# Squares added up on VectorE, norm statistics with tokens on partitions, modulation in pairs of blocks and partly inside the first FFN

## What is computed

```python
def rmsnorm(x, g):
    y = x * lax.rsqrt(jnp.mean(x * x, axis=-1, keepdims=True) + EPS)
    return y * g
def ada_mod(c, w, b, n):
    m = jax.nn.silu(c) @ w + b
    return m.reshape(c.shape[0], n, 1, D_MODEL)
# in every layer, m = ada_mod(...)
h = rmsnorm(x, g[0]) * (1.0 + m[:, 1]) + m[:, 0]
o = rglru_block(h, ...) or nsa_mix(h, ...)          # ends with a projection
x = x + m[:, 2] * rmsnorm(o, g[1])
h = rmsnorm(x, g[2]) * (1.0 + m[:, 4]) + m[:, 3]
o = conv_ffn(h, ...)                                # ends with a projection
x = x + m[:, 5] * rmsnorm(o, g[3])
```

## Time and profile before

| | us |
|---|---|
| median of three runs | 3645.05 (3637.66 to 3645.62) |
| the profiled execution | 3638.49 |
| its span | 3636.6 |
| PE, DVE, POOL, ACT busy | 3221.3, 1728.4, 1113.0, 968.8 |

### The profile page before, as it was taken

How to read it: one execution, slowest core, us unless ns; L and a number is a source line. 1 busy time by engine, 2 the same in 40 slices (tenths; PEclk the granted TensorE clock), 3 DMA queues, 4 the chain that set the end, 5 groups by cost and what they waited for, 6 DMA issues and landing times. The chain is left out here.

```text
span 3636.6 us, 58098 instructions
## 1 busy us (share of the span) xinstructions
PE 3221.3 (89%) x23056; PEld 2903.7 (80%) x23056; DVE 1728.4 (48%) x3136; ACT 968.8 (27%) x1534; POOL 1113.0 (31%) x799
## 2 busy tenths in 40 slices
PE   6886979999999988879767999889787999999986
PEld 5885959999999986879644666566677999999985
DVE  4666046454454445331278888700126454454454
ACT  4544033121121113112123777600123111111111
POOL 1232203333333331223012555400222333333330
PEclk9997989999999998999888999999899999999998
DMA  4213431111111124421242000066202111111112
GB/s 182 74 49 106 153 140 63 47 47 47 47 47 47 47 90 147 155 93 35 70 128 78 2 2 2 2 217 218 88 18 87 48 47 49 44 47 47 47 56 87
DMA packets 75786, 272.89 MB, mean 75 GB/s; under 512 B 9306, under 2 KB 19938, under 8 KB 73330
## 3 DMA queue, kind: packets, MB, share of 16 engines
q1 hardware_dynamic: 73810, 262.99, 20.9%
q10 hardware_dynamic: 1728, 6.34, 0.4%
HBM read 245.47 MB, written 33.10 MB: 77 GB/s over the span
## 5 line engine op out<-in xcount | busy, mean ns | idle before, releaser
L1424 POOL TENSOR_TENSOR w_hi<-w_raw,misc 128x1024 fp32r<-128x1024 f32 x197 | 381.8, 1938 | 2042.9 <-DMA w_raw<-in_w 780.3
L1426 POOL TENSOR_TENSOR w_lo<-w_raw,w_hi 128x1024 fp32r<-128x1024 f32 x197 | 496.6, 2521 | 28.4 <-issue 0.4
L1629 PE MATMUL PA<-hB_hi,w_hi 128*128 128x344 f32 x1512 | 327.5, 325 | 48.4 <-DVE hB_lo L613 23.2
L1629 PE MATMUL PB<-hB_hi,w_hi 128*128 128x344 f32 x1488 | 318.2, 322 | 20.6 <-DVE hB_lo L1813 18.0
L1629 PE MATMUL PB<-hB_lo,w_hi 128*128 128x344 f32 x1488 | 316.8, 321 | 18.0 <-POOL w_lo L1426 18.0
L1629 PE MATMUL PA<-hB_lo,w_hi 128*128 128x344 f32 x1512 | 324.2, 323 | 0.0
L1629 PE MATMUL PA<-hB_hi,w_lo 128*128 128x344 f32 x1416 | 301.5, 322 | 0.0
L1629 PEld LDWEIGHTS PA<-hB_hi,w_hi 128*128 128x128 f32 x1512 | 256.7, 190 | 54.7 <-issue 23.7
L385 DVE SCALAR_TENSOR_TENSOR zb<-ub,vec,zb 128x1024 f32<-128x1024 f32 x48 | 157.9, 3289 | 294.5 <-ACT zb L357 294.5
L1629 PE MATMUL PB<-hB_hi,w_lo 128*128 128x344 f32 x1392 | 294.3, 320 | 0.0
L1629 PEld LDWEIGHTS PB<-hB_hi,w_hi 128*128 128x128 f32 x1488 | 250.9, 189 | 24.1 <-issue 18.2
(11 more groups left out here) (439 smaller groups left out, 6368.7 us busy)
## 6 DMA issues: line engine op xcount, KB each, us to landing
w_raw<-in_w SPq DMA_DIRECT2D x197, 512.0 KB, 3.5
pages<-in_pages SPq DMA_DIRECT2D x64, 384.0 KB, 4.2
cosT<-in_mw SPq DMA_DIRECT2D x32, 512.0 KB, 3.5
sinT<-in_mw SPq DMA_DIRECT2D x32, 512.0 KB, 4.4
mt<-in_mw SPq DMA_DIRECT2D x32, 512.0 KB, 3.9
x_dram<-X SPq DMA_DIRECT2D x3, 4128.0 KB, 12.1
X<-x_dram SPq DMA_DIRECT2D x3, 4128.0 KB, 13.3
mw<-in_mw SPq DMA_DIRECT2D x4, 2048.0 KB, 22.6
```

Source lines behind the costliest of these rows:

```text
L1424: pool.tensor_tensor(w_hi[b], w_raw[b], zero.broadcast_to([P, 1024]), ALU.add)
L1426: pool.tensor_tensor(w_lo[b], w_raw[b], w_hi[b].bitcast(F32), ALU.subtract).then_inc(sem("w_split"), 1)
L1629: mm = pe.matmul(PS[ps][:, c, 0:CH], w[:, w0:w0 + P], x[:, k, c * CH:(c + 1) * CH], start=(k == 0 and n == 0), stop=(k == K - 1 and n == 2))
```

## The change

The odd norms are redone. ACT squares each output block as it comes (`square`, straight from PSUM in the two projections), DVE adds the squares to one accumulator (`acc_add`), and after the last block PE multiplies 9 chunks of 128 tokens of the accumulator with one column of ones (`stats`). The sums then stand with tokens on partitions, 128x9 elements; root and reciprocal are taken of these, and nine transposes of a broadcast column spread them over the partitions in PSUM, from where `residual` reads them. The even norms stay.

Modulation goes in pairs of blocks: one load of 1 MB, passes of 256 columns, one ACT copy, two folds. There is one load buffer and one row buffer. Pairs 0 to 7 run in the LRU loop, 8 to 11 after the first four tiles of the LRU's output projection, 12 to 31 in FFN 0 (one after each pair of up tiles, chunks 0 to 4), 32 to 47 in stage C. The window after the LRU loop and those around norms 1 to 4 go.

The weight loads of the LRU loop are issued a turn ahead. Stage C works only on the 8(i+1) blocks of 64 that query tile i can see, clears the rest of its buffers once, and takes the guard against an empty sum for i = 0 alone. The five copies are issued by ACT after stage C. `ident` is loaded at the start.

```diff
-    def rows_of(pe, e, landed, bank, cs=csil, tiles=mt):
-        pe.wait_ge(sem(f"mt_in{e}"), landed)
+    def rows_of(pe, landed, bank, cs=csil, tiles=mt):
+        pe.wait_ge(sem("mt_in"), landed)
         for k in range(KT):
             q = 32 * (k % 4)
-            mm = pe.matmul(bank[q:q + 32, 0:P], cs[:, NC * k:NC * k + 32], tiles[e][:, k * P:(k + 1) * P],
-                           start=(k < 4), stop=(k >= 4), skip_group_check=True)
+            mm = pe.matmul(bank[q:q + 32, 0:2 * P].rearrange("p (e n) -> p e n", n=P), cs[:, NC * k:NC * k + 32],
+                           tiles[:, :, k * P:(k + 1) * P], start=(k < 4), stop=(k >= 4), skip_group_check=True)
...
+    def ffn_mod(pe, c, p):
+        n = c * PAIRS + (p + 12)
+        pe.wait_ge(sem("md_ev"), n)
+        rows_of(pe, n * 16 + 16, PC)
...
+    def mod_load(sp, p, tiles=mt):
+        after(sp, sem("md_rows"), p)
...
+    def square(act, n, k, src):
+        if k >= 3:
+            act.wait_ge(sem("acc_added"), 7 * (n // 2) + k - 2)
+        out = sq_of(n, k)
+        act.activation(c3(out) if src.ndim == 3 else out, src, ACT.Square).then_inc(sem("nsq_ready"), 1)
+    def acc_add(dve, n, k):
+        dve.wait_ge(sem("nsq_ready"), 8 * (n // 2) + k + 1)
+        dve.drain()
+        acc = sq_of(n, 0)
+        dve.tensor_tensor(acc, acc, sq_of(n, k), ALU.add).then_inc(sem("acc_added"), 1)
+    def stats(pe, n, evicted):
+        pe.wait_ge(*evicted)
+        pe.wait_ge(sem("acc_added"), 7 * (n // 2) + 7)
+        for c in range(KT + 1):
+            t = min(c * P, TOK - P)
+            mm = pe.matmul(PA[:, 0, c:c + 1], acc[:, t:t + P], ones[:, 0:1], start=True, stop=True, skip_group_check=True)
+        mm.then_inc(sem("col_sums"), 1)
+        pe.wait_ge(sem("rst_ready"), n // 2 + 1)
+        for c in range(KT + 1):
+            mm = pe.transpose(PB[:, c // 4, c % 4 * P:(c % 4 + 1) * P], rst[:, c:c + 1].broadcast_to([P, P]), ident)
+        mm.then_inc(sem("rms_spread"), 1)
...
         def root(n):
-            act.wait_ge(sem("sq_used"), 8 * n + 8)
-            act.activation(c3(rms), PA[:, :, 0:CH], ACT.Sqrt, bias=deps).then_inc(sem("sqrt_done"), 1)
+            act.wait_ge(sem("col_sums"), n // 2 + 1)
+            act.activation(rst, PA[:, 0, 0:KT + 1], ACT.Sqrt, bias=deps).then_inc(sem("sqrt_done"), 1)
...
-                    dve.tensor_tensor(b[f"t{k % 2}_{NREG[n]}"][:, 0:NPR], src[:, k, 0:NPR], rms[:, 0:NPR], ALU.mult)
+                    dve.tensor_tensor(b[f"t{k % 2}_{NREG[n]}"][:, 0:NPR], src[:, k, 0:NPR], flat(PB[:, 0:2, :]), ALU.mult)
...
+                for p in range(1, PAIRS):
+                    stream(t0 + 2 * p, t0 + 2 * p + 2)
+                    mod_load(sp, 12 + p)
+                def chunk(c):
+                    for n in range(12):
+                        tile_load((c - 1) * 12 + (t0 + 8 + n), n % 2)
+                        if n in (1, 3, 9, 11):
+                            mod_load(sp, c * PAIRS + (12 + (1, 3, 9, 11).index(n)))
...
-        for n in ("kwin", "vwin", "lst", "fst0", "fst1"):
-            sp.dma_start(o[n], a[n]).then_inc(sem("out_copy"), 16)
...
+    def seen(i):
+        return 8 * i + 8
...
-            s3 = pb[:, 0:512].rearrange("p (h n) -> p h n", n=64)
+            s3 = blocks(pb[:, 0:512], i)
```

More of the change, by code:

```diff
@@ L268, in rows_of, with fold_of @@
         mm.then_inc(sem("md_rows"), 1)
-    def fold_of(pe, e, evicted, out, rows=mr, f=fold):
+    def fold_of(pe, evicted, out, rows=mr, f=fold):
         pe.wait_ge(sem("md_ev"), evicted)
[L272 to L290, removed]
+        for e in range(2):
+            mm = pe.matmul(out[:, e * NC:(e + 1) * NC], rows[:, e, :], f, start=True, stop=True, skip_group_check=True)
+        mm.then_inc(sem("md_fold"), 1)
+    def ffn_mod(pe, c, p):
+        n = c * PAIRS + (p + 12)
+        pe.wait_ge(sem("md_ev"), n)
+        rows_of(pe, n * 16 + 16, PC)
+        if p == 0 and isinstance(c, int) and c == 0:
+            return
+        if p == 1:
+            pe.wait_ge(sem("md_add"), c + 9)
+        q = (p - 1) % PAIRS
+        fold_of(pe, n, PD[:, 2 * q * NC:2 * (q + 1) * NC])
@@ L291, in add_bias, with row_out @@
+    def row_out(act, p, bank, rows=mr):
+        act.wait_ge(sem("md_rows"), p + 1)
+        after(act, sem("md_fold"), p)
+        act.activation(rows, bank[:, 0:2 * P].rearrange("p (e n) -> p e n", n=P), ACT.Copy).then_inc(sem("md_ev"), 1)
+    def add_bias(dve, d0, n, src, folded):
         t = d0 + FIRST
@@ L303, in prepare @@
         dve.drain()
[L305 to L312, removed]
+    def mod_load(sp, p, tiles=mt):
+        after(sp, sem("md_rows"), p)
+        t = p * 2 + FIRST
+        src = a["mw"][t:t + 2] if isinstance(p, int) else a["mw"][ds(t, 2)]
+        sp.dma_start(tiles, src.rearrange("t p n -> p t n")).then_inc(sem("mt_in"), 16)
     def v(name, c):
@@ L1398, in _ @@
         sp.wait_ge(sem("csil_kept"), 1)
-        mod_loads(sp, 64, 32, mt2)
+        for p in range(32, 48):
+            mod_load(sp, p, mt2)
         smp_sp(sp)
@@ L1596, in _ @@
         stage_c_act(act)
+        for n in ("kwin", "vwin", "lst", "fst0", "fst1"):
+            act.dma_start(o[n], a[n]).then_inc(sem("out_copy"), 16)
         att_act(act)
         smp_act(act)
-        evacuate(O1, 141, 93, KT)
-        squares(5, O1, (sem("ev_act"), 93), True)
+        for n in range(KT):
+            act.wait_ge(sem("tile_done"), 141 + n + 1)
+            square(act, 5, n, PS[(141 + n) % 2][:, :, 0:CH])
+            act.activation(c3(O1[:, n, :]), PS[(141 + n) % 2][:, :, 0:CH], ACT.Copy).then_inc(sem("ev_act"), 1)
+        root(5)
         squares(6, X, (sem("x_ready"), 16), True)
@@ L1603, in _, with sums @@
         ffn_act(act, 1)
-        squares(7, O0, (sem("ev_dve"), 48 + CHUNKS * 8 - 8), True)
+        for k in range(KT):
+            act.wait_ge(sem("ev_dve"), 48 + CHUNKS * 8 - 8 + k + 1)
+            square(act, 7, k, O0[:, k, :])
+        root(7)
     @block.tensor
     def _(pe):
-        def sums(n, free=None):
-            if free:
-                pe.wait_ge(*free)
+        def sums(n):
             for k in range(KT):
-                pe.wait_ge(sem("sq_ready"), 8 * n + k + 1)
+                pe.wait_ge(sem("sq_ready"), 4 * n + k + 1)
                 b = NB[NREG[n]][f"sq{k % 2}_{NREG[n]}"]
@@ L1930, in _ @@
         smp_dve(dve)
+        for k in range(1, KT):
+            acc_add(dve, 5, k)
         residual(2, 5, O1, 8)
```

273 lines of the change are left out of this document (140 added, 133 removed).

## The result

The changed kernel takes 3550.48 us, the median of four runs (3545.2 to 3552.13), against 3644.38 for the kernel before in the same comparison: a ratio of 0.9744, 95% interval 0.9727 to 0.976. It is 94 us faster. The forecast was 3528 with a range of 3498 to 3568: the time lies in the range, 22 us above the forecast. It is not in the band of 3515 to 3541, which had the largest chance, 0.45, but in the next one, 3541 to 3572, which had 0.32. The profiled execution took 3550.26, its span 3548.5, 88.1 less than the span before; the forecast had 113.

A forecast was written before the change was run, and what follows sets the result against it. PE, busy 3221 of 3637 us, was taken as the bound, with gains where it isn't busy. Terms summed to −113: 3638.5 to 3525, or 3528 as a median of runs; range 3498 to 3568.

The forecast's parts named there:

- the next one, 3541 to 3572: Whole kernel: terms held by what is next, or FFN pairs dear, put the time at 3541 to 3572; chance 0.32.
- LRU loop, start of the projection: LRU loop −29, its last turn −1.8, output projection's first tile ending 19 us earlier; 50.0 us less together.
- The step that gave all of the loop's 29 to the loads: LRU loop: weights loaded a turn ahead save 4.86 us in six of eight turns, 29.2 us.
- The new wait, +9.5: LRU output projection, after its second tile: PE idles 8 us for pair 9 behind X's reload, plus 1.6 at lower clock.
- Norms: Norms 1, 3, 5, 7: the new chain shortens the way from last tile to first use, 52.4 us less in all.
- The 65 ns more: Norms: by the Trainium skill's rule, 64 operations reading PSUM cost 65 ns more each, 4 us; the sum took 0.
- FFN 0, +36: FFN 0: twenty modulation pairs lie whole on PE's path at 1.8 us each, 36 us more; bounds 26 to 58.
- The rival that put each pair at its upper bound: FFN 0: pairs cost 2.9 us instead of 1.8, 3550 in all; chance 0.32, shared with terms held by what is next.
- the slower rival: FFN 0: modulation loads hold up weights, 6.5 us a pair, twenty times, 130 us more, 3658 in all; chance 0.05.
- KV: KV projection: PE's 7.77 us wait for weights behind five copies on SP and a slow first tile go, −10.4 us.
- Stage C, −26: Stage C, paced by DVE: smaller operations save 1.6 us in each of 16 units, 26 us; bounds 32 and 5.
- After stage C, 0: Attention: copies issued ahead of it on ACT's queue cost 0, upper bound 2 us, since the DMA share is 0.05.

The follow-up runs named there:

- an edit above: Three separate edits to the changed kernel in FFN 0: first two pairs' loads later, 3546.09 us; fourth pair's rows between its tiles, 3544.89; 80 inert waits (40 instructions) ahead, 3540.4.
- the repeats: The kernel before and the changed kernel, each profiled once more with nothing changed: 3646.18 and 3554.58 us.

## Why the prediction was right, and where it was not

**LRU loop, start of the projection.** Right in sum: turns of 29.32 us, as forecast, and the first tile ends 49.2 earlier (50.0 by the terms of the sum). The step that gave all of the loop's 29 to the loads was too much by a third: putting them back cost 19.9.

**The new wait, +9.5.** It was 1.4, with no lower clock after it, against 8 and 1.6. The picture of loads that land in turn held: X, issued at 327.3, landed at 339.5, and the load of pair 9, issued at 330.2, landed 13.1 later, 3.8 behind X, where the forecast had 4.5. Two other sizes were off. X was issued 1.6 us after the second small output (325.66 to 327.27) and not 4.6 (363.58 to 368.20 before), so it and what stood behind it landed 3 to 4 us earlier. And PE came to pair 9 some 3 us later than forecast, 16.8 after `s_lo` and not 14: the first tile's last k-step ran at the lower clock (1.06 for three passes), and the first rows took 1.94.

**Norms.** 52.1 of 52.4. The nine one-column passes ran at the lower clock and took 3.74 to 3.97, 4.5 assumed; DVE's last add took 1.97 instead of 1.23 in norms 1 and 5, beside POOL's split. In norm 3, beside it too, the last two took 5.05, which is why norm 3 gave 8.3 and not 10.2; in norm 7, where POOL has nothing to split, the last two took 2.56. Reading the factor from PSUM costs nothing: `t` takes 1.21 to 1.22 us, and took 1225 ns before. The 65 ns more that the prediction set against the change did not come, and there are 32 such operations, not 64.

**FFN 0, +36.** The pairs were forecast well, 1.8 against 1.64 measured each. What failed is the premise that 20 pairs are all that comes in: the term is 50.4, since two turns of PE's loop cost 9.7 each, where they had cost one wait of about 1 each before. Small passes last ahead of the branch, loads issued at that moment and the place of the loop's head each have a share, and each was taken out by an edit above. The rival that put each pair at its upper bound named 3550, and 3550.48 was measured; that was luck, since the pairs cost less than forecast. No wait for `w_lo` came in FFN 0, so the slower rival's mechanism did not occur.

**KV.** 10.4 exactly, but only 5 of it by the cause that was named.

**Stage C, −26.** It was 15.9. DVE's own time fell as forecast, by 26.6 or 1.66 a unit, but the sizes gave the stage 21.6, and 5.8 went back to what else is new there. With the smaller sizes the single load buffer, which had stood among the bounds and not in the sum, makes PE wait 8.2, and without its reloads the stage was 7.8 shorter. The estimate of 1.6 a unit assumed that DVE would stay the bound; with DVE faster PE has more to do than DVE, at a granted clock between 0.64 and 0.77. One small slip in the working: by its row a reduction of 512 columns in 0.686 us gives 0.30 for 224 columns less, not 0.23.

**After stage C, 0.** The copies cost the rotation and the attention nothing, as forecast. 7.9 more were measured in that stretch in one pair of profiles. 5.4 of them are rotation and attention, of which the repeats leave about 3, and 1.6 are PE's wait ahead of the O projection (19.6 us, 18.0 before). Their cause stays open.

**The whole.** The terms that came out worse than forecast, FFN 0, stage C and what follows it, add up to some 32 us, and the new wait that hardly came gives 8 back. The range held because it was wide enough for that, not because the misses were foreseen.

## What to carry to other kernels

Work put into a stage that one engine bounds costs its own time and also what it does to that engine's loop: keep a large operation, not small ones, last ahead of the branch, and look for waits for issue at the turns. When the engine that paces a loop is made faster, work out the next one at the clock that it will have, not at the one that it has. A gain taken from a term that several edits share should be split by putting one back, even where the sum is right.

## What was not expected of the hardware

Inert instructions ahead of a loop made the kernel 10 us faster: a jump back on PE cost 2.1 to 2.7 us, or 0.7 to 1.5 with a tile queued before it, and a second wait of 2.0 to 2.5 came at one place of the loop's head, with a second packet of code in the trace; loads of 2 MB at that moment made it 4.3 to 4.9. Written out, the same code cost nothing at the same place. And the same code for stage C took 115 to 125 us, at a granted clock of PE from 0.77 down to 0.64, though DVE's time in it was the same to 0.2.
